# Two-layer hybrid trunk with a top-2-of-8 expert layer: tokens of experts 2 to 7 fetched as rows from DRAM and transposed, in place of gather products on TensorE

## What is computed

```python
def moe_swiglu(x, w_router, we_gate, we_up, we_down):
    logits = (x @ w_router).astype(jnp.float32)
    top_vals, top_idx = lax.top_k(logits, TOP_K)          # TOP_K = 2
    gates = jax.nn.softmax(top_vals, axis=-1)
    combine = jnp.einsum("bske,bsk->bse", jax.nn.one_hot(top_idx, N_EXPERTS, dtype=jnp.float32), gates)
    ...
    for e in range(N_EXPERTS):                            # 8 experts, width 3584
        out = out + combine[..., e:e + 1] * swiglu(x, we_gate[e], we_up[e], we_down[e])
```

## Time and profile before

| | |
|---|---|
| time, median of 3 runs | 1351.92 us (1349.66 to 1352.2) |
| profiled execution: time, span | 1350.81 us, 1348.6 us |
| TensorE (PE) busy | 99% of the span |
| VectorE (DVE) busy | 82% |
| ScalarE (ACT) busy | 68% |
| GpSimd (POOL) busy | 2% |
| moved by DMA | 431.60 MB, 320 GB/s over the span |

### The profile page before, as it was taken

How to read it: one execution, slowest core, us unless ns; L and a number is a source line. 1 busy time by engine, 2 the same in 40 slices (tenths; PEclk the granted TensorE clock), 3 DMA queues, 4 the chain that set the end, 5 groups by cost and what they waited for, 6 DMA issues and landing times.

```text
span 1348.6 us, 16026 instructions
## 1 busy us (share of the span) xinstructions
PE 1333.1 (99%) x6659; PEld 1127.7 (84%) x6659; DVE 1110.4 (82%) x811; ACT 920.9 (68%) x712; POOL 33.6 (2%) x47
## 2 busy tenths in 40 slices
PE   9999999999999999999999999999999999999996
PEld 8988888889888888888888888888888888888885
DVE  5877555587789998888889888888988888888996
ACT  5565444444777777777777777777777777777774
POOL 0100000020000000000000000000000000001100
PEclk9999999999999999999999999999999999999998
DMA  9938555555469999999999999999999999999991
GB/s 325 355 103 281 187 188 187 187 177 200 155 214 395 378 381 379 373 354 368 387 371 378 369 386 361 362 387 364 379 379 375 364 365 373 390 373 389 395 396 71
DMA packets 203234, 431.60 MB, mean 320 GB/s; under 512 B 8037, under 2 KB 50069, under 8 KB 203157
## 3 DMA queue, kind: packets, MB, share of 16 engines
q1 hardware_dynamic: 200464, 421.06, 86.1%
q0 software_dynamic: 2608, 9.44, 2.0%
q10 hardware_dynamic: 84, 0.02, 0.0%
HBM read 425.78 MB, written 4.72 MB: 319 GB/s over the span
## 4 chain that ended last, share of the span: by engine, by line
PE 96%; DVE 3%; issue 0%; ACT 0%; POOL 0%; DVEq 0%; POOLq 0%
PE turn L1347 17%; PE turn L1349 17%; PE turn L1348 17%; PE accp L1347 10%; PE accp L1348 10%; PE accp L1349 10%; PE turn L1459 3%; PE turn L1456 3%; PE accp L1666 2%; PE turn L1458 1%; PE turn L1457 1%; PE accp L1652 1%; PE turn L1363 1%; PE accp L1389 0%; DVE x L859 0%
## 5 line engine op out<-in xcount | busy, mean ns | idle before, releaser
L813 DVE TENSOR_TENSOR w_lo<-raw,w_hi 128x2048 fp32r<-128x2048 f32 (+1 forms) x401 | 905.8, 2269 | 150.1 <-ACT w_hi L505 148.4
L505 ACT CAST w_hi<-raw 128x2048 fp32r<-128x2048 f32 x395 | 755.7, 1916 | 208.0 <-PE turn L1349 107.9
L1347 PE MATMUL turn<-w_hi,a_hi 128*128 128x512 f32 x664 | 262.7, 396 | 0.4 <-DVE w_lo L813 0.4
L1349 PE MATMUL turn<-w_hi,a_lo 128*128 128x512 f32 x664 | 259.2, 390 | 0.0
L1348 PE MATMUL turn<-w_lo,a_hi 128*128 128x512 f32 x664 | 258.8, 390 | 0.0
L1347 PE MATMUL accp<-w_hi,hT_hi 128*128 128x512 f32 x448 | 174.8, 390 | 0.0
L1348 PE MATMUL accp<-w_lo,hT_hi 128*128 128x512 f32 x448 | 174.5, 390 | 0.0
L1349 PE MATMUL accp<-w_hi,hT_lo 128*128 128x512 f32 x448 | 174.4, 389 | 0.0
L1349 PEld LDWEIGHTS turn<-w_hi,a_lo 128*128 128x128 f32 x664 | 124.7, 188 | 26.6
L1347 PEld LDWEIGHTS turn<-w_hi,a_hi 128*128 128x128 f32 x664 | 124.8, 188 | 25.2 <-DVE w_lo L813 0.8
L1348 PEld LDWEIGHTS turn<-w_lo,a_hi 128*128 128x128 f32 x664 | 124.9, 188 | 24.7
(11 more groups left out here) (240 smaller groups left out, 1478.2 us busy)
## 6 DMA issues: line engine op xcount, KB each, us to landing
raw<-in_we_gate SPq DMA_DIRECT2D x112, 1024.0 KB, 7.4
raw<-in_we_up SPq DMA_DIRECT2D x112, 1024.0 KB, 7.7
raw<-in_we_down SPq DMA_DIRECT2D x112, 1024.0 KB, 7.5
raw<-in_w_in SPq DMA_DIRECT2D x18, 1024.0 KB, 8.8
raw<-in_w_down SPq DMA_DIRECT2D x11, 1024.0 KB, 5.0
raw<-in_w_gate SPq DMA_DIRECT2D x10, 1024.0 KB, 5.2
raw<-in_w_up SPq DMA_DIRECT2D x10, 1024.0 KB, 5.2
raw<-in_w_out SPq DMA_DIRECT2D x8, 1024.0 KB, 9.8
```

Of the source, the lines that this page charges most:

```text
L505: nc.scalar.copy(w_hi[:, p % PARTS, :], raw[:, p % RING, :]).then_inc(hi_done, 1)
L813: return nc.vector.tensor_tensor(out, whole, hi.bitcast(f32), ALU.subtract)
L1347: nc.tensor.matmul(to, lh, rh, start=start, stop=False, **group)
L1349: return nc.tensor.matmul(to, ll, rh, start=False, stop=stop, **group)
```

## The change

After the last layer norm before the experts, GpSimd writes the 256 token rows of `x` to DRAM (`token_rows`). For each pair of experts, TensorE multiplies `pick` with the token numbers (`token_ids`, two equal columns of float32r), so that each slot gets its token's number (`sum_tokens`, after the up product of step 0 of experts 1, 3 and 5). VectorE casts the numbers to integers (`token_of`). GpSimd fetches the 128 rows of one expert by indirect DMA into `more_rows` (`fetch_tokens`); a slot without a token fetches row 0, where its column was zero before. In steps 3 and 4 of experts 1 to 6, TensorE transposes four blocks of `more_rows` each (`turn_tokens`), ScalarE rounds them (`round_tokens`) and VectorE subtracts (`rest_of_tokens`). Two buffers of `xg_hi` and `xg_lo` are left; `third_hi` and `third_lo` are gone. The transposes of the last pair's `pick` move from step 3 to step 5 of expert 6.

```diff
@@ buffers and constants @@
+        token_of = numbers[:, 8:8 + E]
+        token_ids = sb("token_ids", [P, NT, 2], f32r)
-        third_hi = sb("third_hi", [P, KD, P], f32r)
-        third_lo = sb("third_lo", [P, KD, P], f32r)
+        token_rows = nc.dram_tensor("token_rows", [TOK, D], f32, kind="Internal").ap()
-        misc_pair = accp[:, 3, :].rearrange("p (k i t) -> p k i t", k=2, i=2)
+        misc_tokens = accp[:, 3, :].rearrange("p (k t) -> p k t", t=P)
-        PAIR = {(0, 0): 0, (3, 0): 1, (3, 1): 2, (4, 0): 3, (4, 1): 4, (5, 0): 5, (5, 1): 6, (6, 0): 7}
-        def gather_at(e, s, place):
-            if e % 2 and e < E - 1 and (s, place) in PAIR:
-                return e + 1, PAIR[s, place]
-            return None
+        def half_of(e, b):
+            return 2 * (e - 2) + b
+        def tokens_at(e, s):
+            return (e + 1, s - 3) if s in (3, 4) and 0 < e < E - 1 else None
@@ GpSimd @@
+                nc.gpsimd.iota(ids_whole, pattern=[[P, NT], [0, 2]], base=0, channel_multiplier=1,
+                               allow_small_or_imprecise_dtypes=True)
-            for e in range(E - 1):
+            def write_rows(e):
                 pool.wait_ge(ys_kept, e + 1)
                 pool.dma_start(slot_rows[e * P:(e + 1) * P, :], ys_rows[:]).then_inc(ys_written, 16)
+            def fetch_tokens(e):
+                pool.wait_ge(tokens_known, e // 2)
+                if e == 2:
+                    pool.wait_ge(tokens_written, 16 * NT)
+                else:
+                    pool.wait_ge(xg_turned, half_of(e, 0))
+                nc.gpsimd.indirect_dma_start(more_rows[:], None, token_rows, bass.IndirectOffsetOnAxis(
+                    ap=token_of[:, e:e + 1], axis=0)).then_inc(tokens_loaded, 16)
+            for n in range(NT):
+                pool.dma_start(token_rows[n * P:(n + 1) * P, :], x[:, n, :]).then_inc(tokens_written, 16)
+            for e in range(E - 1):
+                write_rows(e)
+                if e % 2 == 0 and e + 3 < E:
+                    fetch_tokens(e + 2)
+                    fetch_tokens(e + 3)
@@ ScalarE @@
-            def copy_tokens(e, j):
-                act.wait_ge(xg_piece, copied(e - 1) + j + 1)
-                ks = slice(2 * (j % 4), 2 * (j % 4) + 2)
-                for i in range(2):
-                    to = (xg_hi, xg_lo)[j // 4][(e + i) % 3]
-                    last = nc.scalar.copy(to[:, ks, :], misc_pair[:, :, i, :])
-                last.then_inc(xg_copied, 1)
+            def round_tokens(e, half):
+                act.wait_ge(xg_turned, half_of(e, half) + 1)
+                nc.scalar.copy(xg_hi[e % 2][:, 4 * half:4 * half + 4, :], misc_tokens).then_inc(xg_rounded, 1)
...
                         act.wait_ge(x_lo_ready, NT + 1)
+                        act.wait_ge(tokens_written, 16 * NT)
                         nc.scalar.activation(x[:, n, :], x[:, n, :], ACT.Copy, scale=ALPHA).then_inc(acc_added, 1)
@@ VectorE @@
+                    nc.vector.tensor_copy(token_ids[:], ids_whole)
...
+            def rest_of_tokens(e, half):
+                dve.wait_ge(xg_rounded, half_of(e, half) + 1)
+                ks = slice(4 * half, 4 * half + 4)
+                rest_of(xg_lo[e % 2][:, ks, :], misc_tokens, xg_hi[e % 2][:, ks, :]).then_inc(xg_done, 1)
...
+                if s == 0 and e % 2 and e < E - 1:
+                    dve.wait_ge(tokens_summed, (e + 1) // 2)
+                    nc.vector.tensor_copy(token_of[:, e + 1:e + 3], accp[:, 3, 0:4:2]).then_inc(tokens_known, 1)
+                at = tokens_at(e, s)
+                if at is not None:
+                    rest_of_tokens(*at)
@@ TensorE @@
-            def gather_piece(e, j):
+            def sum_tokens(e):
                 pe.wait_ge(pick_ready, e + 2)
-                if copied(e - 1) + j:
-                    pe.wait_ge(xg_copied, copied(e - 1) + j)
-                k0 = 2 * (j % 4)
-                gather((x_hi, x_lo)[j // 4], misc_pair, k0, k0 + 2, slice(0, 2)).then_inc(xg_piece, 1)
+                if e > 2:
+                    pe.wait_ge(xg_done, half_of(e, 0))
+                for i in range(2):
+                    for n in range(NT):
+                        last = nc.tensor.matmul(accp[:, 3, 2 * i:2 * i + 2], pick[:, n, i, :], token_ids[:, n, :],
+                                                start=(n == 0), stop=(n == NT - 1))
+                last.then_inc(tokens_summed, 1)
+            def turn_tokens(e, half):
+                pe.wait_ge(tokens_loaded, 16 * (e - 1))
+                pe.wait_ge(tokens_known, e // 2)
+                if half_of(e, half):
+                    pe.wait_ge(xg_done, half_of(e, half))
+                for k in range(4):
+                    cols = slice((4 * half + k) * P, (4 * half + k + 1) * P)
+                    last = nc.tensor.transpose(misc_tokens[:, k, :], more_rows[:, cols], ident[:])
+                last.then_inc(xg_turned, 1)
...
-                    pe.wait_ge(xg_copied, copied(i // STEPS))
+                    pe.wait_ge(xg_done, half_of(i // STEPS, 0) + 2)
```

More of the change, by code:

```diff
@@ L108, in hybrid_trunk_kernel @@
         small = sb("small", [P, 208])
-        numbers = sb("numbers", [P, 96], i32)
+        numbers = sb("numbers", [P, 92], i32)
         most_i, rows_of = numbers[0:1, 0:1], numbers[:, 4:8]
+        token_of = numbers[:, 8:8 + E]
+        token_ids = sb("token_ids", [P, NT, 2], f32r)
         with ExitStack() as mixers:
@@ L156, in hybrid_trunk_kernel @@
         before_whole, ones_whole = work[:, 3088:3216], work[:, 3216:3344]
+        ids_whole = work[:, 3344:3344 + 2 * NT].rearrange("p (n i) -> p n i", n=NT)
         centred = y_work[:, :].rearrange("p (n d) -> p n d", n=NT)
@@ L164, in hybrid_trunk_kernel @@
         x_hi, x_lo = (x_both[:, i] for i in range(2))
-        xg_hi, xg_lo = ([two[:, 0], two[:, 1], third[:]] for two, third in (
-            (a[:, :].rearrange("p (i k t) -> p i k t", i=2, k=KD), third)
-            for a, third in ((a_hi, third_hi), (a_lo, third_lo))))
+        xg_hi, xg_lo = ([two[:, 0], two[:, 1]] for two in (
+            a[:, :].rearrange("p (i k t) -> p i k t", i=2, k=KD) for a in (a_hi, a_lo)))
         first_hi_tokens, first_lo_tokens = (
@@ L256, in hybrid_trunk_kernel @@
                              "pick_ready", "x_hi_ready", "x_lo_ready"))
-        gathered, xg_hi_ready, xg_lo_ready, xg_piece, xg_copied = (
-            sem(n) for n in ("gathered", "xg_hi_ready", "xg_lo_ready", "xg_piece", "xg_copied"))
+        gathered, xg_hi_ready, xg_lo_ready, xg_turned, xg_rounded, xg_done = (
+            sem(n) for n in ("gathered", "xg_hi_ready", "xg_lo_ready", "xg_turned", "xg_rounded", "xg_done"))
+        tokens_written, tokens_summed, tokens_known, tokens_loaded = (
+            sem(n) for n in ("tokens_written", "tokens_summed", "tokens_known", "tokens_loaded"))
         slots_written, slots_read = sem("slots_written"), sem("slots_read")
@@ L472, in _ @@
                     layer_norm(2, (ln2_g[1], ln2_b[1]))
-            for e in range(E - 1):
+            def write_rows(e):
                 pool.wait_ge(ys_kept, e + 1)
                 pool.dma_start(slot_rows[e * P:(e + 1) * P, :], ys_rows[:]).then_inc(ys_written, 16)
+            def fetch_tokens(e):
[13 more added lines that the diff above has]
+                    fetch_tokens(e + 3)
             pool.wait_ge(ys_written, 16 * (E - 1))
             pool.wait_ge(rows_chosen, 1)
+            pool.wait_ge(xg_turned, half_of(E, 0))
             for j, (n, k) in enumerate(ROWS):
@@ L691, in copy_pick @@
                 nc.scalar.copy(pickT[:, 1, :], accp[:, 3, TOK:2 * TOK]).then_inc(slots_read, 1)
-            def copy_tokens(e, j):
-                act.wait_ge(xg_piece, copied(e - 1) + j + 1)
-                ks = slice(2 * (j % 4), 2 * (j % 4) + 2)
-                for i in range(2):
-                    to = (xg_hi, xg_lo)[j // 4][(e + i) % 3]
-                    last = nc.scalar.copy(to[:, ks, :], misc_pair[:, :, i, :])
-                last.then_inc(xg_copied, 1)
[L702 to L705, removed]
+            def round_tokens(e, half):
+                act.wait_ge(xg_turned, half_of(e, half) + 1)
+                nc.scalar.copy(xg_hi[e % 2][:, 4 * half:4 * half + 4, :], misc_tokens).then_inc(xg_rounded, 1)
             def after_up(i):
                 e, s = divmod(i, STEPS)
-                if s == 3 and e == E - 2:
+                at = tokens_at(e, s)
+                if at is not None:
+                    round_tokens(*at)
+                if s == 5 and e == E - 2:
                     copy_pick()
-                tokens_at(e, s, 0)
             def after_down(i):
@@ L718, in after_down @@
                     keep_ys(e - 1)
-                tokens_at(e, s, 1)
             for i in range(N_STEPS):
@@ L1229, in after_up @@
                 if s == STEPS - 1 and e % 2 == 0 and e < E - 2:
-                    if e:
-                        dve.wait_ge(xg_piece, copied(e))
                     choose(e + 2)
```

(25 more changed lines are left out.)

2 lines of the change are left out of this document (removed).

## The result

| | before | after |
|---|---|---|
| time, median of 17 runs each, beside each other | 1349.90 us (1349.03 to 1352.2) | 1354.16 us (1352.55 to 1355.84) |
| profiled execution: time, span | 1350.81, 1348.6 us | 1354.25, 1352.5 us |

The ratio is 1.0027, 95% interval 1.002 to 1.0035: the kernel became slower, by 4.3 us from median to median (3.7 between the means), where the forecast was 4.6 us faster. Time, range and sign were wrong.

A forecast was written before the change was run, and what follows sets the result against it. TensorE was taken to bound the kernel, paying one to one in the expert stage. -12.0 + 5.9 + 1.5 = -4.6 us from the median 1351.92 gave 1347.3 us, range 1345.2 to 1349.7.

The forecast's parts named there:

- the sum: TensorE's path in the expert stage: -12.0 for gather pieces, +5.9 for transposes, +1.5 for token sums, -4.6 us in all.
- a plain step stays 16.80: Sign of being right: an expert-stage step with nothing extra keeps its length of 16.80 us.
- rival 2: Row transposes on TensorE cost their record's 0.272 us each, 13.1 us for 48; +2.6 us, 1354.5 us; chance 3%.
- Gather pieces removed, -12.0: Expert stage, TensorE: 24 gather pieces of four matmuls go, at 0.50 us each, saving 12.0 us.
- transposes, 12 x 0.49: Experts 2 to 7, TensorE: 12 added groups of four fp32 transposes at 0.49 us, 5.9 us (5.3 to 6.7).
- token sums, 3 x 0.50: TensorE: three added groups of four matmuls of 2 columns at 0.50 us, 1.5 us (0 to 1.7).
- Rival 4: Gain larger than forecast: both additions on TensorE at their lower ends, -6.7 us, 1345.2 us; chance 3%.
- VectorE's 12 subtractions are hidden: Steps with transposes: VectorE's added 128x512 subtractions, 683 ns each, 8.2 us in all, fit beside TensorE's work.
- Rival 3: A new wait, late subtraction or late copy of x, eats much of the gain: -0.5 or -1.6 us; chance 8%.
- The weight stream has room: Expert stage: the row fetches beside the weight loads cost nothing; if not hidden, 3.1 MB would cost 8.4 us.
- Rival 1: Weight stream has no room, loads landing over 12.5 us after issue: 8.4 us, net +3.8, 1355.7 us; chance 5%.
- The copy of x ends in time: Before the experts: the DRAM write lands by about 382 us, 6.7 us before ScalarE scales x at 388.71.

The follow-up runs named there:

- the second spacer of 32 bytes: The changed kernel with an unused spacer of 32 bytes a partition behind `token_ids`, hT_hi then 64 bytes off; 1354.26 us against 1350.87 for the kernel before, ratio 1.003.

## Why the prediction was wrong

**The step that failed is the sum**, which took the plain step over as it was ("a plain step stays 16.80") and had no term for it. The diff shows a new buffer of 32 bytes in the middle of the list; the prediction costed the move of every buffer behind it at nothing, without a word. Its rivals looked for waits, for the stream's room and for dear transposes, and not one of them was that the untouched matmuls get slower. Of its signs of being wrong (a wait for a split, a step with transposes over 17.5, the scaling of x after 389) none appeared; only the plain step, which it listed among the signs of being right, gave it away. That the measured 1354.16 lies beside rival 2's price of 1354.5 is chance: the transposes cost what the sum says, below. The size, by the traces (first to last transposes of h, where all three kernels have the same steps):

```profile
397.80 0.60 PE L1666 MATMUL accp<-ident,y_work 128*128 128x128 f32 x4
...
1326.10 0.60 PE L1666 MATMUL accp<-ident,y_work 128*128 128x128 f32 x4
```

```profile
397.83 0.60 PE L1688 MATMUL accp<-ident,y_work 128*128 128x128 f32 x4
...
1329.74 0.60 PE L1688 MATMUL accp<-ident,y_work 128*128 128x128 f32 x4
```

Before (the first pair) 928.30 us, after (the second) 931.91, with `token_ids` last 1320.37 - 396.78 = 923.59. The exchange of gather products for transposes is worth 923.59 - 928.30 = -4.7 us; the addresses cost 931.91 - 923.59 = +8.3. Together +3.6, and the medians say +4.3. Between the forecast of 1347.3 and the measured 1354.16 there is one thing more: the forecast started from the median of three runs, 1351.92, and the median of 17 is 1349.90. That base was 2.0 us too high, which hid part of the miss. (The 2.2 us outside the span, taken over too, are 1.75 after the change.)

**The rest of the forecast, by its own steps:**
- *Gather pieces removed, -12.0; transposes, 12 x 0.49; token sums, 3 x 0.50: -4.6.* Measured at the old addresses: 0.49 for four transposes (17.29 - 16.80), 0.50 for a token sum (17.30 - 16.80), -4.7 for all. All three prices were right; the token sum's was a choice between the prices of matmuls of 8 and of 256 columns, with nothing of 2 columns to read. Rival 4, more than the sum, is out too. The rule of the Trainium skill that was weighed, about 275 ns for a transpose ("TensorE: Matmul & The Clock Gate", Part 4), is that of the record here too (271 ns in the row below), but the stream pays 0.12 us for each. Rival 2 is out.

```profile
L825 DVE TENSOR_TENSOR a_lo<-accp,a_hi 128x512 fp32r<-128x512 f32 x12 | 8.2, 681 | 0.0
L1780 PE MATMUL accp<-ident,more_rows 128*128 128x128 f32 x48 | 7.2, 271 | 0.0
L1769 PE MATMUL accp<-token_ids,pick 128*128 128x2 f32 x12 | 1.5, 229 | 0.0
```

- *VectorE's 12 subtractions are hidden.* 681 ns each in the rows above, and TensorE has no wait behind them. Rival 3 is out.
- *The weight stream has room.* Loads issued from 510 to 530 us, over a row write and a fetch, landed in 9.0 us, where the point of decision was 12.5. Rival 1 is out.

```profile
raw<-in_we_gate SPq DMA_DIRECT2D x3, 1024.0 KB, 8.9
raw<-in_we_up SPq DMA_DIRECT2D x2, 1024.0 KB, 9.0
raw<-in_we_down SPq DMA_DIRECT2D x2, 1024.0 KB, 9.0
slot_rows<-ys_rows POOLq DMA_DIRECT2D x1, 512.0 KB, 6.3
more_rows<-token_rows,numbers POOLq DMA_INDIRECT x1, 8.5
```

- *The copy of x ends in time.* Issued at 373.64 and landed in 7.1 us, so near 381; x is scaled at 388.79 (388.71 before) and TensorE's one wait is at 394.97, for 0.35.

```profile
373.64 1.08 POOL L490 DMA_DIRECT2D token_rows<-x  x2
...
388.79 2.01 ACT L747 ACTIVATE x<-x 128x1024 f32<-128x1024 f32 x2
...
394.97 0.50 PE L1369 MATMUL turn<-w_hi,a_hi 128*128 128x512 f32 x1 [0.35 <-DVE w_lo L825]
```

So the mechanism that was argued was there with its size, and 1345.64 us is what the kernel takes with it alone; the range would have held that time. The sum was not wrong in a term, it lacked one.

## What to carry to other kernels

A new buffer, however small, moves every buffer that is allocated behind it, and that is part of a change: put it last, or work out the addresses of the hot matmuls' operands before and after and keep stationary and moving ones at the same place modulo 256 bytes, as far as these runs reach (float32r, 512 columns). When a change that takes work away makes a kernel slower, first measure a stretch that the change doesn't touch (here the plain step): if it is longer, the price of the new instructions can't be the whole cause. And a busy engine without waits is no proof that its work has its usual price.

## What the runs showed of the hardware

**The distance of stationary and moving operands.** These float32r matmuls of 512 columns follow each other every 0.227 us when the start addresses of stationary and moving operands differ by a multiple of 256 bytes (256 and 512 were tried on top of the old distances, which are multiples of 2048) and every 0.233 us at a distance of 32, 64 or 128 bytes: 2.8% of such a product, 0.15 to 0.17 us in 24 matmuls. What in the chip does it was not shown, nor which pair it is (a matmul's own two, or a moving operand and the next stationary one), nor why one part off is nearly as dear as both.

**The clock at the router is not the same in each execution.** The stretch of small matmuls ahead of the experts, 373 to 386 us, in the kernel with `token_ids` last, and in the one with the second spacer of 32 bytes:

```profile
373.00:386.00 13.00, 12.77 (x73) 10.71 (x73) 11.87 (x27) 8.56 (x12) 1.94 (x4) 1.00 0.56 167
```

```profile
373.00:386.00 13.00, 12.77 (x61) 11.40 (x60) 9.22 (x25) 7.35 (x10) 1.54 (x3) 0.74 0.52 161
```

The granted clock is 1.00 in the first (2.4 GHz throughout) and 0.74 in the second, so about half of it was at the lower level, 1.2 GHz; before and after it was 0.87. The kernels have the same work there, and the first transposes of h stand at 396.78 us in the first, at 397.80 before and at 399.18 in the second. Executions of the kernel before itself differ alike: those of 1349.0 us have a mean granted clock of 0.997, those of 1350.8 us 0.996 and those of 1352.2 us 0.994. That the router's stretch makes up all of that difference is not shown, as only one execution of each kernel has a trace. But a single execution says less here than the length of a plain step, which repeats to 0.02 us.
